# A transformer block's first mixer: where the mask is added, where the convolution's taps stand, and the order behind the heads

## The reference

```python
h = rmsnorm(x, norm1_g)
z = h @ w_in + b_in
glu_val, glu_gate, q, k, v, g_conv, g_attn = split(z)
# depthwise convolution over 31 taps, layer norm, SiLU
u = glu_val * sigmoid(glu_gate)
y = depthwise_conv(u, conv_w) + conv_b
conv_out = silu(layernorm(y, ln_g, ln_b)) @ w_conv_out
# 16 heads of 64, 2 key/value heads, a window of 128, blocks of 128 queries
s = where(mask, (rope(q) @ rope(k).T) * 64**-0.5, -1e30)
m = maximum(max(s), sink)
e = exp(s - m)
o = (e / (sum(e) + exp(sink - m))) @ v
attn_out = o @ w_attn_o
x = x + (sigmoid(g_conv) * conv_out + sigmoid(g_attn) * attn_out) @ w_out
```

## Time and profile before

| | |
|---|---|
| median of 3 runs | 3579.71 us (3578.02 to 3587.12) |
| the profiled execution | 3577.24 us, its span 3575.4 us |
| TensorE busy | 3457.9 us, 97% of the span |
| VectorE busy | 1979.6 us, 55% |
| ScalarE busy | 1249.0 us, 35% |
| GpSimd busy | 922.8 us, 26% |
| mean granted TensorE clock | 0.988 |

### The profile page before, as it was taken

The page is one execution under the profiler, slowest core; times in us unless marked ns, Lnnn a source line. Parts: engine busy times, 40 slices in busy tenths (PEclk is TensorE's granted clock), DMA queues, the critical chain, the costliest instruction groups (busy, mean ns, idle before and its releaser), DMA issues.

```text
span 3575.4 us, 42970 instructions
## 1 busy us (share of the span) xinstructions
PE 3457.9 (97%) x16542; PEld 2806.1 (78%) x16542; DVE 1979.6 (55%) x3107; ACT 1249.0 (35%) x1821; POOL 922.8 (26%) x390
## 2 busy tenths in 40 slices
PE   7999898999999999999999999999999999999997
PEld 5777676887888888888888887888757888788885
DVE  6889855877888898322222226320458766632205
ACT  3234433222333333332222324332344656233223
POOL 0010143443000000244444444444211000444441
PEclk9999999999999999999999999999999999999998
DMA  3211132333555554655555553222312222322222
GB/s 109 89 53 43 58 107 95 119 123 118 171 165 168 195 186 165 235 190 197 190 194 189 191 200 104 99 95 95 119 59 77 71 83 71 112 94 95 95 94 83
DMA packets 144359, 446.75 MB, mean 125 GB/s; under 512 B 12776, under 2 KB 45928, under 8 KB 139936
## 3 DMA queue, kind: packets, MB, share of 16 engines
q1 hardware_dynamic: 108304, 405.26, 32.9%
q10 hardware_dynamic: 35856, 38.75, 3.1%
HBM read 372.64 MB, written 71.32 MB: 124 GB/s over the span
## 4 chain that ended last, share of the span: by engine, by line
PE 85%; DVE 10%; DVEq 2%; issue 1%; ACT 1%; POOL 1%; DMA 0%; POOLq 0%; SPq 0%; ACTq 0%
PE ps L212 52%; PE ps L1001 19%; PE ps L1254 6%; DVE conv_out L726 3%; PE ps L984 2%; DVEq L719 1%; DVE m_gates L1950 1%; PE ps L1508 1%; DVE norm_r L301 1%; PE ps L1452 1%; POOL slot_parts L200 1%; DVE stats L785 1%; PE ps L1591 1%; PE ps L231 0%; PE ps L1574 0%
## 5 line engine op out<-in xcount | busy, mean ns | idle before, releaser
L212 PE MATMUL ps<-h_norm_hi,slot_parts 128*128 128x512 f32 x4752 | 1524.8, 397 | 38.8 <-POOL slot_parts L200 10.0
L200 POOL TENSOR_TENSOR slot_parts<-ring,slot_parts 128x1024 fp32r<-128x1024 f32 x373 | 905.8, 2430 | 2315.8 <-ACT slot_parts L196 2315.8
L212 PEld LDWEIGHTS ps<-h_norm_hi,slot_parts 128*128 128x128 f32 x4752 | 896.8, 189 | 246.9 <-issue 20.4
L212 PE MATMUL ps<-x_low,slot_parts 128*128 128x512 f32 x2312 | 902.4, 390 | 0.0
L196 ACT ACTIVATE slot_parts<-ring 128x1024 fp32r<-128x1024 f32 x558 | 586.8, 1052 | 487.4 <-DMA ring<-in_stream 294.6
L1001 PE MATMUL ps<-gated_hi,slot_parts 128*128 128x512 f32 x2048 | 630.9, 389 | 1.5 <-POOL slot_parts L200 1.5
L212 PEld LDWEIGHTS ps<-x_low,slot_parts 128*128 128x128 f32 x2312 | 437.7, 189 | 92.9 <-issue 2.2
L1001 PEld LDWEIGHTS ps<-gated_hi,slot_parts 128*128 128x128 f32 x2048 | 384.5, 188 | 81.6 <-POOL slot_parts L200 1.9
L1001 PE MATMUL ps<-gated_lo,slot_parts 128*128 128x512 f32 x1024 | 398.4, 389 | 0.0
L1186 DVE TENSOR_TENSOR gated<-gates_back,experts_back 128x512 f32<-128x512 f32 x128 | 95.1, 744 | 495.1 <-DMA experts_back<-experts_dram 485.1
L200 DVE TENSOR_TENSOR slot_parts<-ring,slot_parts 128x1024 fp32r<-128x1024 f32 x185 | 227.5, 1230 | 136.2 <-ACT slot_parts L196 131.3
(11 more groups left out here) (357 smaller groups left out, 3361.5 us busy)
## 6 DMA issues: line engine op xcount, KB each, us to landing
ring<-in_stream SPq DMA_DIRECT2D x560, 512.0 KB, 3.3
experts_dram<-experts SPq DMA_DIRECT2D x64, 512.0 KB, 4.7
gates_dram<-gates_by_key ACTq DMA_DIRECT2D x32, 1024.0 KB, 10.6
gates_back<-gates_dram SPq DMA_DIRECT2D x32, 1024.0 KB, 4.7
experts_back<-experts_dram SPq DMA_DIRECT2D x64, 512.0 KB, 5.0
x_res<-in_xT SPq DMA_DIRECT2D x2, 2048.0 KB, 9.9
x_dram<-x_res SPq DMA_DIRECT2D x4, 512.0 KB, 3.2
bias_by_distance<-bias_rows_dram ACTq DMA_DIRECT2D x8, 256.0 KB, 4.1
```

What stands on the lines that cost most here:

```text
L200: e.tensor_tensor(to[:, BUFFER[n], 1, :], ring[:, n % RING, :], to[:, BUFFER[n], 0, :].bitcast(F32), ALU.subtract).then_inc(s_lo, 1)
L212: mm = e.matmul(psum, w2[wv][:, k, :], x2[xv], start=start and v == 0, stop=stop and v == 2)
```

## The change

- The mask is kept in bf16. Four matmuls per tile, with a bf16 identity as the stationary operand, put it into the score banks (`start=True`), and the scores are accumulated on top. VectorE takes the maximum straight from PSUM, unscaled; the factor 64**-0.5 goes into the small operation behind it and into the exponential's `scale`. ScalarE's exponential reads PSUM. The operation that wrote scaled and masked scores to SBUF is gone.
- The rotation of the next tile's queries stands between the transposes of the two heads; the turn of the last tile's output stands behind them; PV goes to banks 4 and 5.
- The taps are given out anew, with eight ahead of the V tokens; the first four tiles are finished first; the sums over the tiles (now in their own buffer, `conv_sum`) are given out like taps. All of them end within tile 7.
- The splits of the gate slots move: slot `n_g` ahead of the V tokens and K's rope, slot `n_g + 2t + 1` behind the rope. VectorE, not GpSimd, splits slot `n_ao + 2`.
- The first mean stands ahead of product 2 instead of behind it, the second behind product 4 instead of 5. The sigmoids of the convolution's gates stand between ScalarE's squares. `gate_attended` and the slots' rounding are put elsewhere accordingly.

The core of the diff:

```diff
-    M = sb(m, "band_mask", [P, NB, 2 * P])
+    M = sb(m, "band_mask", [P, NB, 2 * P], BF16)
+    ident_b = sb(m, "ident_bf16", [P, P], BF16)
+    neg_sinks = sb(m, "minus_sinks", [P, HEADS])
+    M_in = G[:, 0:2, :].rearrange("p a s -> p (a s)")
+    conv_sum = sb(m, "conv_sum", [P, S])
-    bv = sb(m, "b_v", [P, P])
+    bv = osb[:, 0, :]
-    BESIDE_GLU, BESIDE_Q, BEFORE_ROPE, AFTER_ROPE, AFTER_MAX = 10, 5, 4, 4, 7
+    BESIDE_GLU, BESIDE_Q, BEFORE_V_TOKENS, BEFORE_ROPE, AFTER_ROPE, AFTER_MAX = 9, 5, 8, 4, 5, 8
...
-        some(KT * TAPS, KT)
-        return order
+        some(BESIDE_Q * (n_g - n_q - 1) + BEFORE_V_TOKENS, KT)
+        some(KT // 2 * TAPS - sum(done[:KT // 2]), KT // 2)
+        late = [(c, w) for w in range(TAPS) for c in range(KT // 2, KT) if w >= done[c]]
+        sums = [(c, TAPS) for c in range(1, KT // 2)]
+        order += late[:2] + sums[:1] + late[2:4] + sums[1:2] + late[4:6] + sums[2:] + late[6:]
+        return order + [(c, TAPS) for c in range(KT // 2, KT)]
...
+        def q_rot(t):
+            e.matmul(PS[:, 6, :], rot, Q[:, t, :], start=True, stop=True).then_inc(at_rot, 1)
+
+        q_rot(0)
         for g, t, b in HEAD_TILES:
-            after(e, at_on, 2 * t - 1)
-            e.matmul(PS[:, 6, :], rot, Q[:, t, :], start=True, stop=True).then_inc(at_rot, 1)
             gate_gemm(t, 0)
-            if t:
-                o_turn(t - 1)
-            else:
+            if t == 0:
                 e.wait_ge(k_done, 4)
+            for h in range(2):
+                after(e, at_oe if h else at_pt, t - 1 if h else 2 * t)
+                for c in range(2):
+                    e.matmul(PS[:, 2 * h + c, :], ident_b[:, :],
+                             M[:, 2 * c:2 * c + 2, :].rearrange("p n k -> p (n k)"), start=True, stop=False)
             e.wait_ge(at_qr, t + 1)
             for h in range(2):
-                after(e, at_oe if h else at_pt, t if h else 2 * t)
...
-                                  start=True, stop=True)
+                                  start=False, stop=n % 2 == 1)
...
                 e.wait_ge(at_ex, 2 * t + h + 1)
+                if h == 0:
+                    after(e, at_on, 2 * t)
...
+                if h == 0 and t + 1 < KT:
+                    q_rot(t + 1)
+                if h == 1 and t:
+                    o_turn(t - 1)
...
-        attn_out(1, range(KT - 1))
+        attn_out(1, range(4))
         attn_out(0, range(KT - 1, KT))
-        attn_out(1, range(KT - 1, KT))
+        attn_out(1, range(4, KT))
         e.wait_ge(at_oe, KT)
+        e.wait_ge(ln_in, 1)
+        e.matmul(PS[:, 5, :], mean, conv_sum[:, :], start=True, stop=True).then_inc(ln_mu, 1)
         for t in range(2, KT):
             after(e, m1_gated, t - 3)
             attn_out(t, range(KT))
-            if t == 2:
-                e.wait_ge(ln_in, 1)
-                e.matmul(PS[:, 5, :], mean, ra[:, :], start=True, stop=True).then_inc(ln_mu, 1)
-            if t == 5:
+            if t == 4:
                 e.wait_ge(ln_sum, KT)
                 e.matmul(PS[:, 6, :], mean, rb[:, :], start=True, stop=True).then_inc(ln_mm, 1)
-        e.wait_ge(m1_gated, KT)
         for t in range(KT):
             w2 = slot_tiles(e, n_co + t)
+            if t < 4:
+                e.wait_ge(m1_gated, KT - 3 + t)
...
         for g, t, b in HEAD_TILES:
             gate(t, 0)
-            if t:
-                attended(t - 1)
...
-                    e.activation(Sb[:, h, n, :], Sb[:, h, n, :], ACT.Exp, bias=st[:, h, 1, n:n + 1],
+                    e.activation(Sb[:, h, n, :], PS[:, 2 * h + n // 2, (n % 2) * 256:(n % 2) * 256 + 256],
+                                 ACT.Exp, bias=st[:, h, 1, n:n + 1], scale=HD ** -0.5,
                                  accum_out=st[:, h, 3, n:n + 1])
...
+        slot_hi(e, n_ao + 2)
         for t in range(KT):
             e.activation(X[:, t, :], X[:, t, :], ACT.Sigmoid).then_inc(m1_sg, 1)
-        for n in range(2, 4):
-            slot_hi(e, n_ao + n)
-        for t in range(KT):
-            e.activation(G[:, t, :], G[:, t, :], ACT.Sigmoid).then_inc(m1_sg, 1)
-        slot_hi(e, n_ao + 4)
+            if t == 3:
+                slot_hi(e, n_ao + 3)
         for c in range(KT):
             e.wait_ge(ln_xc, c + 1)
             after(e, ln_sum, c - 1)
             e.activation(qr[:, c % 2, :], Y[:, c, :], ACT.Square).then_inc(ln_sq, 1)
+            e.activation(G[:, c, :], G[:, c, :], ACT.Sigmoid).then_inc(m1_sg, 1)
             if c == 3:
-                slot_hi(e, n_ao + 5)
+                slot_hi(e, n_ao + 4)
+        slot_hi(e, n_ao + 5)
         slot_hi(e, n_ao + 6)
...
-            if c == 3:
+            if c == 2:
                 slot_hi(e, n_co)
...
+            if p == 0:
+                e.tensor_copy(M[:, :, :].rearrange("p n k -> p (n k)"), M_in)
+                e.tensor_copy(ident_b[:, :], ident)
+                e.tensor_scalar(neg_sinks[:, :], sinks[:, :], -1.0, None, ALU.mult)
...
+        slot_lo(e, n_g)
+        at = taps(at, BEFORE_V_TOKENS)
         e.wait_ge(slot_done, n_kv + 3)
...
-        slot_lo(e, n_g)
-        slot_lo(e, n_g + 1)
         for g, t, b in HEAD_TILES:
-            if t:
-                slot_lo(e, n_g + 2 * t + 1)
-            if t >= 2:
-                attended_lo(e, t - 2)
             at = taps(at, BEFORE_ROPE if t else 0)
...
+            slot_lo(e, n_g + 2 * t + 1)
             at = taps(at, AFTER_ROPE)
...
-                e.scalar_tensor_tensor(
-                    out=Sb[:, h, :, :].rearrange("p n k -> p (n k)"),
-                    in0=PS[:, 2 * h:2 * h + 2, :].rearrange("p a b -> p (a b)"),
-                    scalar=HD ** -0.5, in1=M[:, :, :].rearrange("p n k -> p (n k)"),
-                    op0=ALU.mult, op1=ALU.add)
+                e.tensor_reduce(mx, PS[:, 2 * h:2 * h + 2, :].rearrange("p a (n k) -> p (a n) k", n=2), AX.X,
+                                ALU.max)
                 e.drain()
-                e.tensor_reduce(mx, Sb[:, h, :, :], AX.X, ALU.max)
-                e.drain()
-                e.tensor_scalar(nm, mx, sinks[:, 2 * t + h:2 * t + h + 1], -1.0, ALU.max, ALU.mult)
+                e.tensor_scalar(nm, mx, -HD ** -0.5, neg_sinks[:, 2 * t + h:2 * t + h + 1], ALU.mult, ALU.min)
...
             slot_lo(e, n_g + 2 * t + 2)
-            at = taps(at, AFTER_MAX)
+            if t >= 2:
+                attended_lo(e, t - 2)
+            at = taps(at, AFTER_MAX if t < KT - 1 else len(TAP_ORDER) - at)
...
         slot_lo(e, n_ao + 1)
         attended_lo(e, KT - 2)
         attended_lo(e, KT - 1)
-        taps(at, len(TAP_ORDER) - at)
-        e.drain()
-        e.tensor_tensor(ra[:, :], Y[:, 0, :], Y[:, 1, :], ALU.add)
-        for c in range(2, KT):
-            e.drain()
-            ins = e.tensor_tensor(ra[:, :], ra[:, :], Y[:, c, :], ALU.add)
-        ins.then_inc(ln_in, 1)
+        slot_lo(e, n_ao + 2)
```

More of the change, by code:

```diff
@@ L497, in mixer1_pe @@
                     for c in range(2):
-                        mm = e.matmul(PS[:, 3 if h else 6, n * HD:(n + 1) * HD], pT[:, h, 2 * n + c, :],
+                        mm = e.matmul(PS[:, 4 + h, n * HD:(n + 1) * HD], pT[:, h, 2 * n + c, :],
                                       V[:, n + c, g * HD:(g + 1) * HD], start=c == 0, stop=c == 1)
@@ L555, in mixer1_act @@
         e.dma_start(rb[:, :].bitcast(I32), a["positions"].partition_broadcast(P)).then_inc(m1_pos, 16)
-        e.dma_start(M[:, :, :], a["band_mask"]).then_inc(m1_in, 16)
+        e.dma_start(M_in, a["band_mask"].rearrange("p n k -> p (n k)")).then_inc(m1_in, 16)
         e.dma_start(sinks[:, :], a["sinks"].partition_broadcast(P)).then_inc(m1_in, 16)
-        e.dma_start(bv[:, :], a["b_v"].partition_broadcast(P)).then_inc(m1_in, 16)
+        e.dma_start(bv, a["b_v"].partition_broadcast(P)).then_inc(m1_in, 16)
         e.wait_ge(s_const, CONST_IN)
@@ L617, in mixer1_act @@
             gate(t, 1)
-            if 0 < t < KT - 1:
+            if t:
+                attended(t - 1)
                 attended_hi(t - 1)
-        attended_hi(KT - 2)
         attended(KT - 1)
@@ L676, in mixer1_pool @@
                 cosine(t + 1)
-        e.wait_ge(s_lo, ORDINAL[n_ao + 2])
-        for n in range(n_ao + 2, n_wo + KT):
+        e.wait_ge(s_lo, ORDINAL[n_ao + 3])
+        for n in range(n_ao + 3, n_wo + KT):
             slot_lo(e, n)
@@ L717, in taps @@
             for c, w in TAP_ORDER[at:at + n]:
-                if c in fresh or at == 0 or not fresh:
+                if c in fresh or at == 0 or not fresh or w == TAPS and "sum" in fresh:
                     e.drain()
@@ L721, in taps @@
                 fresh.add(c)
-                if w == 0:
+                if w == TAPS:
+                    fresh.add("sum")
+                    ins = e.tensor_tensor(conv_sum[:, :], Y[:, 0, :] if c == 1 else conv_sum[:, :], Y[:, c, :],
+                                          ALU.add)
+                    if c == KT - 1:
+                        ins.then_inc(ln_in, 1)
+                elif w == 0:
```

(28 more changed lines are left out.)

## The result

The changed kernel takes 3549.6 us, the median of four executions (3549.1 to 3550.1), where the kernel before, run beside it, takes 3578.9 (3577.8 to 3587.1). The ratio is 0.9914, with a 95% interval from 0.9900 to 0.9929: faster by 29.2 us. The forecast was 3557 us in a range of 3546 to 3569, faster. The side and the range were right, and 7 us of gain were missing from the forecast.

The account below looks back on a forecast made before the run. VectorE was taken to bound the head loop, TensorE the stretches before and after. 0.5 + 8.6 + 13.8 + 1.5 = 24.4 us, less 2 for hand-offs, gave 3554.8; plus 2.5 for the median, 3557 us, range 3546 to 3569.

Parts of the forecast that it names:

- Before the loop: Ahead of the head loop: 0.5 us won of TensorE's 2.9 us wait for the last gated input tile.
- The first gate product: Ahead of the head loop: its weight split moves earlier, so it starts at 203.55 and ends at 209.05 us, 5.8 us won.
- The loop: Head loop: VectorE's tile falls from 24.09 to 23.2 us, TensorE's is 22.8; 8.6 us won, the 5.8 included.
- After the loop: Behind the heads: waits for the sum and GpSimd's split and the hole before conv_out go; 51.1 for 64.9 us, 13.8 won.
- the rule on the port: VectorE instructions with two SBUF inputs are blocked by GpSimd reading SBUF, others not; the 2.7 us would shrink by about 1.
- The first conv_out product: Behind the mixer's heads: it runs warm, 2.1 us taken back and 0.6 given for the second slot, 1.5 us won.
- Hand-offs: No particular place: 2 us given back for hand-offs between engines that the forecast set to nothing.
- Medians: Whole kernel: the median of the runs shown, 3579.7 us, lies 2.5 us above the profiled execution.
- A: Behind the loop: TensorE stops for sum of squares and slots behind sigmoids; 13.8 becomes about 5, 3566 us; chance 0.17.
- B: Head loop: dear mask matmuls make TensorE the bound, from 1.03 us each; 3579 us (chance 0.05) or slower, 3591 (0.03).
- C: Head loop: TensorE's waits only move, 24 us per tile remain, 4 us beyond the head start lost; 3561 us; chance 0.15.
- The two rules: Skill's rules: VectorE from PSUM costs 62 cycles more, estimated 0.065 us per maximum; GpSimd reading SBUF blocks two-SBUF-input VectorE instructions.

Follow-up runs that it names:

- one tap less: Changed kernel with one tap left out in each of head tiles 0 to 6 (seven of 248 taps not computed): 3547.5 us, ratio 0.9903.
- three repairs: Changed kernel with last gated input tile before its five taps, four last sums behind attended tile 6's split, second conv_out slot split by VectorE: 3546.6 us, 0.9904.

## Why the prediction was right, and where its sizes were off

**Before the loop: 0.5 forecast, 0.6 measured.** As said: the wait on the last gated tile went from 2.9 to 2.3 us. That the K rotation starts 0.6 us earlier too is partly luck: behind that hole the clock fell alike in both profiles (0.57 and 0.58 from 132 to 136 us), while other kernels with the same edits there start it up to 2.7 us earlier than the changed kernel.

**The first gate product: right.** It started at 202.40 us, 5.3 before the 207.70 of the earlier trace rows, and ended at 208.31 for my 209.05. Undone alone it costs 5.0 us in the loop, for my 5.8.

**The loop: 8.6 forecast, 13.6 measured. This is the term that was mis-sized.** The mechanism held, shown by two runs: VectorE leads (25.8 us lost when it gets the mask back), and TensorE has room for the masks (twice the masks, 1.7 us). The 5.0 us lie in three steps.
- The tile of VectorE was put at 23.2 us and is 22.9: from the end of tile 0 to the end of tile 6 it is 136.7 us for my 138.6, 1.9 us. Most of it is the collision with GpSimd. I kept its 1.06 us; the five taps that it meets now take 4.40 us, and 3.56 where GpSimd does nothing, so 0.84.
- VectorE's end of tile 0 was put at 227.7 us and is 225.76, of which 0.6 is the earlier start: 1.3 us. The forecast let it hang on TensorE: PV to 226.0, then 1.7 for the divisions. PV ended at 224.2, and VectorE works without a wait from 207.19 us on, so that its own work ends the tile; with the masks twice, the first maximum still starts 13.3 us behind the K rotation. TensorE's tile I had put at 22.8 us, and it needs 21.95. I had taken pieces of the earlier trace rows with TensorE's small pauses in them, such as 3.58 us for the scores; from start to start, in tile 0 after, the scores take 212.44 - 209.18 = 3.26.
- "TensorE ends tile 7 some 21.5 us after VectorE's end of tile 6" was 19.8: 1.7 us. I had put the collision into tile 7 too, but the last tile has no next queries for GpSimd to multiply. From the last division to the first maximum are 371.57 - 362.5 = 9.1 us for my 10.3.

The three are 1.9 + 1.3 + 1.7 = 4.9 of the 5.0. VectorE of the changed kernel in order of time: five taps behind the split, in tile 7 without and in tile 1 with GpSimd beside them.

```profile
368.09 3.56 DVE L750 SCALAR_TENSOR_TENSOR conv_out<-conv_in,cst,conv_out 128x512 f32<-128x512 f32 x5
```

```profile
230.04 1.22 DVE L200 TENSOR_TENSOR slot_parts<-ring,slot_parts 128x1024 fp32r<-128x1024 f32 x1
231.35 4.40 DVE L750 SCALAR_TENSOR_TENSOR conv_out<-conv_in,cst,conv_out 128x512 f32<-128x512 f32 x5
```

**After the loop: 13.8 forecast, 13.7 measured**, with the parts near what I gave them: 1.6 us of wait for attended tile 6 (1.2), 2.0 us at products 4 and 5 (2.7), both for GpSimd's slots, none at the second mean. By the rule on the port the 2.7 should have shrunk by about 1; they did by 0.7. Where it comes from is shown by two runs: with the taps of before the stretch is 13.0 longer, with the norm's order of before 8.6. The sum of both is more than the gain, since each edit alone moves the wait only as far as the other lets it.

**The first conv_out product: 1.5 forecast, 0.2 measured.** The product does run warm, as the clock of 1.00 up to 441.3 us shows. But the second slot's split is GpSimd's and ends 1.7 us after TensorE wants it (441.26); I had given 0.6 for that. With the split on VectorE the hole is 0.6 and the stretch 1.1 us shorter.

**Hand-offs: 2 given back, 0.7 measured**, and those in the rest, which no edit touches. They aren't the DMA wait of the expert layer, though it is 9.9 us and was 9.1: TensorE's next wait, for a split of GpSimd's, ends 27.4 us after the second norm's start in both (at 580.01 us before and 551.92 after), and the 0.7 us come up more than 2500 us behind the second norm's start; why stays open. The 2 us were a deduction without a place, and no place asked for them. Medians: the one of before lies 1.6 us over its profiled execution's time, where I had 2.5, and that of after at its own, which is the other 1.8 us between 27.4 and 29.2.

**Rivals.** A, the gain behind the loop given back: refuted, no wait at the second mean. B, a dear mask matmul: refuted, 0.218 us where it decides from 1.03. C, nothing in the loop beyond the head start: refuted by the pickups, 22.9 us for 24.09. Its price was wrong by the forecast's own sum: beyond the 5.8 us of head start the loop was to give 2.8 us, not 4, which makes it 3560 us.

**The two rules.** The maximum from PSUM has a mean of 1217 ns over 16, in the view by form, and the same operation from SBUF took 1.22 us:

```profile
L804 DVE TENSOR_REDUCE stats<-ps 128x4 f32<-128x1024 f32 x16 | 19.5, 1217 | 0.0
```

The surcharge that the Trainium skill (VectorE: DVE Perf Modes, the table of the trn2 errata) names, an estimate of 0.065 us each, does not show here: the trace disagrees. The port shows more clearly than I had it. GpSimd split a slot from 406.06 to 408.83 us, and VectorE's operations beside it were (changed kernel, in order of time):

```profile
406.50 0.68 DVE L847 TENSOR_TENSOR conv_out<-conv_out,ps 128x512 f32<-128x512 f32 x1
407.28 2.11 DVE L842 TENSOR_TENSOR rope_b<-rope_b,q_roped 128x512 f32<-128x512 f32 x1
409.31 0.68 DVE L847 TENSOR_TENSOR conv_out<-conv_out,ps 128x512 f32<-128x512 f32 x1
```

The centring (line 847), which has its mean in PSUM, took 0.68 us beside GpSimd and 0.68 without it; the addition of squares (line 842), with both operands in SBUF, took 2.11 instead of 0.69 and ended at 409.39, 0.56 us after GpSimd, about its own length. That is the rule of the Trainium skill (SBUF — State Buffer, Who interferes with whom), and the trace agrees.

## What to carry to other kernels

When one engine leads a loop by less than a microsecond, price an edit on both engines, from start to start and not by durations, and look at the last pass through the loop by itself: what it has no need of is missing from its collisions too. A deferred heap of work before a single waiting instruction costs there what nothing ahead of that instruction covers: 15.4 us with the mean ahead of product 2, 4.2 with it behind, as before. The same work spread where the engine is idle costs next to nothing, and spread where it leads it costs itself: here 5.2 us of loop. After a rearrangement, read the small waits that remain and ask which of them stands behind work that another place could take; three such moves and ten taps moved to an idle stretch gave 10.8 us in the medians, over a third of what the change had given, though some 2 us of it may be the clock's.

## What the runs showed of the hardware that was not expected

- The same hole had two outcomes for the clock. At 129 us TensorE waits 2.3 us for the last gated tile in the changed kernel and in the run with one tap less, with equal work ahead of it. The busy time by stretch of the changed kernel, 126 to 136 us:

```profile
126.00:132.00 6.00, 3.70 (x17) 2.73 (x16) 5.61 (x8) 1.06 (x1) 0.00 (x0) 1.00 0.35 115
132.00:136.00 4.00, 4.00 (x11) 3.12 (x12) 3.68 (x5) 0.00 (x0) 0.00 (x0) 0.58 0.05 19
```

and of the run with one tap less:

```profile
126.00:132.00 6.00, 3.70 (x17) 2.71 (x16) 5.61 (x8) 1.06 (x1) 0.00 (x0) 1.00 0.26 87
132.00:136.00 4.00, 4.00 (x19) 3.30 (x18) 3.45 (x5) 0.00 (x0) 0.00 (x0) 1.00 0.00 0
```

  The clock is 0.58 in one and 1.00 in the other, that is, in the first TensorE works at 1.2 GHz for most of the 4 us. Seven kernels, in eight profiles, have this hole and the same work up to it. Their clock from 132 to 136 us lies anywhere from 0.58 to 1.00, but the whole ten microseconds show only two outcomes, 0.83 in six profiles and 1.00 in two (the changed kernel, then the one with one tap less):

```profile
126.00:136.00 10.00, 7.70 (x27) 5.85 (x26) 9.29 (x12) 1.06 (x1) 0.00 (x0) 0.83 0.23 77
```

```profile
126.00:136.00 10.00, 7.70 (x34) 6.01 (x33) 9.06 (x12) 1.06 (x1) 0.00 (x0) 1.00 0.16 52
```

  What varies among the six is where the slower stretch lies. From the end of the hole to the K rotation it is 68.2 to 68.4 us in them and 66.8 in the two others, so the fall costs some 1.5 us. The rest of the 2.7 us between the starts of the K rotation (200.2 to 197.5 us) was there before the hole, which ends between 131.8 and 130.4 us; there too the clock differs, from 0.67 in the changed kernel to 0.74 in the run with one tap less, over the stretch from 30 to 50 us. Two executions of the changed kernel had 0.58 and 0.61, so that it may hang on the kernel rather than on chance; that stays open. The holes of 1.0 to 1.7 us behind the heads did not lower it.
- The same behind the mixer, where it costs more. Behind the second norm's start the changed kernel and the one with three repairs wait for the same things on TensorE, 44.0 us in all in the first and 43.0 in the second, whose DMA wait of the expert layer is shorter (9.0 for 9.9 us). Yet ScalarE's copies of TensorE's products, matched one by one, show the second falling behind in four steps: by 1.6 us between 26 and 33 us after that start, by 0.8 at some 330, by 1.1 between 2041 and 2051 and by 1.0 between 2176 and 2182; 0.5 us is made up at the end. At the first and the last of the steps (26 to 36 and 2175 to 2185 us after that start) the changed kernel has:

```profile
550.51:560.51 10.00, 8.59 (x37) 7.05 (x38) 0.00 (x0) 4.04 (x5) 4.91 (x3) 1.00 0.35 108
2699.51:2709.51 10.00, 9.33 (x48) 7.79 (x47) 8.94 (x11) 5.05 (x9) 0.00 (x0) 1.00 0.17 53
```

  and the one with three repairs:

```profile
543.49:553.49 10.00, 8.59 (x31) 6.91 (x32) 0.00 (x0) 2.49 (x4) 3.74 (x2) 0.83 0.22 62
2692.49:2702.49 10.00, 7.73 (x33) 6.00 (x32) 8.33 (x11) 5.47 (x9) 0.00 (x0) 0.83 0.17 53
```

  The clock is 1.00 in one and 0.83 in the other. So 3 to 4 us between two kernels of this program can be the clock's alone: over all profiles the rest lies between 3022.8 and 3027.5 us. It is why the repairs show only 3 us in the medians, as far as one profile of each can tell.
- A collision of VectorE and GpSimd costs both. GpSimd's product of 1.27 us takes 2.18 us now that it starts just behind the start of VectorE's split, which itself isn't delayed (1.22 us); the taps behind it are, by 0.84.
- Exponentials that read PSUM have a mean of 483 ns where those from SBUF had 497; with the reads of their sums behind them they are busy for 43.3 us in all, for 43.8: no loss from the other memory.
